# RWKV scan: both products of a block-inversion level over two PSUM banks, and the factor turned by transposes instead of kept twice

## The reference, cut to what matters

```python
def _rwkv7_scan(r, w, k, v, kk, a):
    def step(S, inp):
        r_t, w_t, k_t, v_t, kk_t, a_t = inp
        sa = -jnp.einsum('nhvk,nhk->nhv', S, kk_t)
        S = S * w_t[:, :, None, :] + sa[..., None] * (kk_t * a_t)[:, :, None, :] + v_t[..., None] * k_t[:, :, None, :]
        return S, jnp.einsum('nhvk,nhk->nhv', S, r_t)
    S0 = jnp.zeros((n, h, dk, dk), r.dtype)
    ...
    _, y = lax.scan(step, S0, xs)
```

## Time and profile before

| | us |
|---|---|
| median of 3 runs | 4701.57 |
| lowest and highest | 4696.87, 4706.41 |
| the profiled execution | 4681.85 |
| its span, first to last instruction | 4679.7 |
| granted TensorE clock, mean over the span | 0.946 |

### The profile page before, as it was taken

The page is one execution under the profiler, slowest core; times in us unless marked ns, Lnnn a source line. Parts: engine busy times, 40 slices in busy tenths (PEclk is TensorE's granted clock), DMA queues, the critical chain, the costliest instruction groups (busy, mean ns, idle before and its releaser), DMA issues. The chain is left out here.

```text
span 4679.7 us, 68997 instructions
## 1 busy us (share of the span) xinstructions
PE 4174.6 (89%) x28006; PEld 2421.8 (52%) x28006; DVE 1989.1 (43%) x3941; ACT 1353.8 (29%) x3154; POOL 519.1 (11%) x535
## 2 busy tenths in 40 slices
PE   5999889999998999999997765888798799999994
PEld 2455466644444666445546654777675344433341
DVE  1455256612563565235204665777356222222224
ACT  2125345511144554123113444443141111111110
POOL 0000000000000000000000002322003322222220
PEclk8999999999999999999998886999898899999997
DMA  5122330031222402422011003000304679999995
GB/s 194 46 79 72 105 122 24 31 131 52 91 82 82 132 18 102 158 81 94 26 63 55 2 8 109 3 3 3 117 1 166 241 252 303 309 328 334 333 332 152
DMA packets 199189, 565.69 MB, mean 121 GB/s; under 512 B 24450, under 2 KB 115187, under 8 KB 185427
## 3 DMA queue, kind: packets, MB, share of 16 engines
q1 hardware_dynamic: 162450, 441.90, 26.3%
q0 software_dynamic: 36416, 119.29, 9.3%
HBM read 437.02 MB, written 124.11 MB: 120 GB/s over the span
## 5 line engine op out<-in xcount | busy, mean ns | idle before, releaser
L729 PE MATMUL banks<-arena 128*128 128x512 f32 (+1 forms) x2928 | 1122.3, 540 | 8.1 <-ACT arena L584 5.7
L729 PEld LDWEIGHTS banks<-arena 128*128 128x128 f32 x2928 | 555.3, 191 | 534.1 <-issue 497.8
L3267 PE MATMUL banks<-arena 128*32 128x512 f32 (+2 forms) x2896 | 561.6, 595 | 4.2 <-DMA arena<-in_experts 3.3
L1250 PE MATMUL banks<-arena 128*128 128x256 f32 (+1 forms) x1152 | 375.8, 481 | 18.8 <-DMA arena<-y_d 14.5
L3267 PEld LDWEIGHTS banks<-arena 128*32 128x32 f32 (+2 forms) x2896 | 198.6, 130 | 358.3 <-issue 354.5
L1469 PE MATMUL banks<-arena 96*128 96x512 f32 (+1 forms) x800 | 329.3, 547 | 34.3 <-DMA arena<-k_d 21.1
L1520 DVE TENSOR_REDUCE arena<-banks 128x1 f32<-128x512 f32 (+1 forms) x400 | 226.7, 593 | 294.8 <-PE banks L1469 294.7
L1250 PEld LDWEIGHTS banks<-arena 128*128 128x128 f32 x1152 | 221.4, 193 | 164.5 <-issue 145.2
L3286 PE MATMUL banks<-arena 128*32 128x512 f32 (+2 forms) x1448 | 286.4, 595 | 1.7 <-DVE arena L3316 1.2
L3351 ACT ACTIVATE arena<-banks 128x256 f32<-128x256 f32 x79 | 30.5, 386 | 781.9 <-PE banks L3267 781.9
L3234 POOL DMA_INDIRECT r_d<-arena x125 | 181.5, 1452 | 639.2 <-DVE arena L3316 530.3
(11 more groups left out here) (500 smaller groups left out, 5635.4 us busy)
## 6 DMA issues: line engine op xcount, KB each, us to landing
arena<-in_experts SPq DMA_DIRECT2D x64, 3072.0 KB, 13.2
arena<-in_ada_w SPq DMA_DIRECT2D x12, 2048.0 KB, 7.6
arena<-in_w_in SPq DMA_DIRECT2D x23, 1024.0 KB, 5.6
arena<-in_w_mod SPq DMA_DIRECT2D x8, 2048.0 KB, 17.3
arena<-in_w_out SPq DMA_DIRECT2D x6, 2048.0 KB, 11.4
arena<-in_w_in SPq DMA_DIRECT2D x5, 2048.0 KB, 7.9
arena<-in_tokens SPq DMA_DIRECT2D x4, 2048.0 KB, 17.9
arena<-in_w_mod SPq DMA_DIRECT2D x8, 1024.0 KB, 5.1
```

What stands on the lines that cost most here:

```text
L729: i = e.matmul(self.out_of(n), lhs, rhs, start=k == 0, stop=k == KT - 1)
L1250: i = e.matmul(bank(n % 4)[:, 0:nn], w[:, q, :], H[:, q, t0:t0 + nn], start=q == 0, stop=q == KT - 1)
L3267: op = e.matmul(ABK[(q - q0) % 2][rows, :], xT[(q - q0) % 2][:, P * k:P * k + P][:, rows], weights[:, i % SLOTS, 512 * k:512 * k + 512], s ...
```

## The change

It replaces the pair of factors by one and turns it when needed.

- VectorE keeps only the turned factor `TT_` (256 columns): L2489, L2491 and L2497 work on 256 columns at every level. L2497's result is read from two banks, and its operands are viewed so that the bank index comes first.
- At each level TensorE first transposes `TT_` by two 128x128 transposes, each into columns 128 to 255 of one of the lane's two banks; these wait for the factor, the products behind them also for GpSimd's mask. The eight products with `am` follow, into columns 0 to 127: the chunk (row half) picks the bank, the head's parity the partition half.
- ScalarE's copy takes columns 0 to 255 of both banks at once (128x512 where it was 128x256) into `XN`, which thus holds the product and the plain factor.
- The second product is eight block products for every level (sixteen before, but for the last level), with the row half picking the bank, into columns 256 to 383. The second update is gone.
- X1's product moves from behind the second product of level 2 to behind the first product of level 4, one round later, and writes columns 256 to 511 of both banks, the bank by chunk. Its copy becomes two copies of 64x256, which now stand ahead of the level's copy on ScalarE.
- The uses of the banks are dealt out anew: first and second product each take both banks.

The masks on GpSimd, the Gram products, L2431, L2437 and the chain part are as before, and so is `staged`'s order otherwise.

```diff
--- before.py
+++ after.py
@@ -2321,8 +2321,9 @@
                 self.AB, self.BQ = al(512), al(768)
                 self.AN = self.AB[:, 256:512]
                 self.BT, self.QK_, self.QB = (self.BQ[:, 256 * j:256 * j + 256] for j in range(3))
-                self.TTN, self.XX = al(512), al(256)
-                self.TT_, self.TN = self.TTN[:, 0:256], self.TTN[:, 256:512]
+                self.TT_, self.XN = al(256), al(512)
+                self.banks = [bank(2 * i), bank(2 * i + 1)]
+                self.both = ps[:, 1024 * i:1024 * i + 1024].rearrange("p (two n) -> p two n", two=2)
                 self.am = [al(256), al(256)]
                 self.WT, self.X1, self.UB, self.q1 = (al(256) for _ in range(4))
                 self.WTv = z3(self.WT)
@@ -2335,10 +2336,18 @@
                     for q in range(2):
                         give("gram", n, q, 0), give("gram", n, q, 1)
                     for s_ in LEVELS:
-                        give("x", n, s_), give("tt", n, s_)
-                        if s_ == 2:
-                            give("x1", n)
+                        give("x", n, s_, 0), give("x", n, s_, 1), give("tt", n, s_, 0), give("tt", n, s_, 1)
                     give("wt", n, 0), give("wt", n, 1)
+
+            def product(self, c, h):
+
+                o = 256 * c + 64 * (h // 2)
+                return self.XN[half[h % 2], o:o + 64]
+
+            def factor(self, c, h):
+
+                o = 256 * (h // 2) + 128 + 64 * c
+                return self.XN[half[h % 2], o:o + 64]
 
         lanes = [lane(i) for i in range(3)]
 
@@ -2391,36 +2400,36 @@
                 op.then_inc(Tn.hit("gram", n, gi), 1)
                 yield
             for li, s_ in enumerate(LEVELS):
-                o = sl.of("x", n, s_)
-                sl.free(e, Vn, Sn, "x", n, s_)
                 AM = b.am[li % 2]
+                assert sl.of("x", n, s_, 0) is b.sl.banks[0] and sl.of("tt", n, s_, 0) is b.sl.banks[0]
+                for c in range(2):
+                    sl.free(e, Vn, Sn, "x", n, s_, c)
                 e.wait_ge(*Vn.at("tt", n, li))
+                for g in range(2):
+                    op = e.transpose(b.banks[g][:, P:2 * P], b.TT_[:, P * g:P * g + P], ident)
                 e.wait_ge(*Gn.at("am", n, li))
-                for h in range(4):
-                    hs_ = slice(64 * h, 64 * h + 64)
-                    for tp in half:
-                        op = e.matmul(o[tp, hs_], AM[tp, hs_], b.TT_[tp, hs_], start=True, stop=True)
+                for g in range(2):
+                    for pa in range(2):
+                        hs_ = slice(128 * g + 64 * pa, 128 * g + 64 * pa + 64)
+                        for c, tp in enumerate(half):
+                            op = e.matmul(b.banks[c][half[pa], 64 * g:64 * g + 64], AM[tp, hs_], b.TT_[tp, hs_], start=True, stop=True)
                 op.then_inc(Tn.hit("x", n, li), 1)
-                yield
-                o = sl.of("tt", n, s_)
-                sl.free(e, Vn, Sn, "tt", n, s_)
-                e.wait_ge(*Sn.at("free", "x", n, s_))
-                for lhs, rhs, c0 in ((b.TN, b.XX, 0), (b.XX, b.TN, 256))[0:2 if s_ < 32 else 1]:
-                    for h in range(4):
-                        hs_ = slice(64 * h, 64 * h + 64)
-                        for tp in half:
-                            op = e.matmul(o[tp, c0 + 64 * h:c0 + 64 * h + 64], lhs[tp, hs_], rhs[tp, hs_], start=True, stop=True)
-                op.then_inc(Tn.hit("tt", n, s_), 1)
-                if s_ == 2:
-                    o = sl.of("x1", n)
-                    sl.free(e, Vn, Sn, "x1", n)
+                if s_ == 4:
                     there(e, n)
                     e.wait_ge(*Vn.at("free", "gram", n, 1, 1))
                     for h in range(4):
                         hs_ = slice(64 * h, 64 * h + 64)
-                        for tp in half:
-                            op = e.matmul(o[tp, hs_], b.BT[tp, hs_], v[tp, hs_], start=True, stop=True)
+                        for c, tp in enumerate(half):
+                            op = e.matmul(b.banks[c][tp, 256 + 64 * h:320 + 64 * h], b.BT[tp, hs_], v[tp, hs_], start=True, stop=True)
                     op.then_inc(Tn.hit("x1", n), 1)
+                yield
+                for pa in range(2):
+                    sl.free(e, Vn, Sn, "tt", n, s_, pa)
+                for g in range(2):
+                    for c in range(2):
+                        for pa in range(2):
+                            op = e.matmul(b.banks[pa][half[c], 256 + 64 * g:320 + 64 * g], b.factor(c, 2 * g + pa), b.product(c, 2 * g + pa), start=True, stop=True)
+                op.then_inc(Tn.hit("tt", n, s_), 1)
                 yield
             e.wait_ge(*Vn.at("tt", n, 5))
             for c in range(2):
@@ -2484,17 +2493,18 @@
                     e.tensor_tensor(dst[:, pa], sl.of("gram", n, gi, pa)[:, 0:P * w_].rearrange("p (q g n) -> p q g n", q=w_, g=2), msk, ALU.mult).then_inc(Vn.hit("free", "gram", n, gi, pa), 1)
                 if gi == 0:
                     o_ = CONST + cat["lv1"][0] + (0 if f else 64)
-                    lv = ar[:, o_:o_ + 128].rearrange("p (q n) -> p q n", q=2).unsqueeze(2).broadcast_to([P, 2, 4, 64])
+                    lv = ar[:, o_:o_ + 64].unsqueeze(1).broadcast_to([P, 4, 64])
                     e.wait_ge(*Vn.own())
-                    e.tensor_tensor(b.TTN.rearrange("p (q h n) -> p q h n", q=2, h=4), b.AB.rearrange("p (q h n) -> p q h n", q=2, h=4), lv, ALU.mult).then_inc(Vn.hit(), 1)
+                    e.tensor_tensor(h64(b.TT_), h64(b.AB[:, 0:256]), lv, ALU.mult).then_inc(Vn.hit(), 1)
                     e.wait_ge(*Vn.own())
-                    e.tensor_tensor(h64(b.TTN), cm("id64").unsqueeze(1).broadcast_to([P, 8, 64]), h64(b.TTN), ALU.subtract).then_inc(Vn.hit("tt", n, 0), 1)
+                    e.tensor_tensor(h64(b.TT_), cm("id64").unsqueeze(1).broadcast_to([P, 4, 64]), h64(b.TT_), ALU.subtract).then_inc(Vn.hit("tt", n, 0), 1)
                 yield
             for li, s_ in enumerate(LEVELS):
                 yield
-                w_ = 512 if s_ < 32 else 256
+                tt = b.TT_.rearrange("p (g two n) -> p two g n", g=2, two=2)
                 e.wait_ge(*Tn.at("tt", n, s_))
-                e.tensor_tensor(b.TTN[:, 0:w_], b.TTN[:, 0:w_], sl.of("tt", n, s_)[:, 0:w_], ALU.subtract).then_inc(Vn.hit("free", "tt", n, s_), 1)
+                e.tensor_tensor(tt, tt, b.both[:, :, 256:384].rearrange("p two (g n) -> p two g n", g=2), ALU.subtract).then_inc(Vn.hit("free", "tt", n, s_, 0), 1)
+                Vn.note("free", "tt", n, s_, 1)
                 Vn.note("tt", n, li + 1)
                 yield
             yield
@@ -2529,11 +2539,13 @@
             yield
             for li, s_ in enumerate(LEVELS):
                 e.wait_ge(*Tn.at("x", n, li))
-                e.activation(b.XX, sl.of("x", n, s_)[:, 0:256], ACT.Copy).then_inc(Sn.hit("free", "x", n, s_), 1)
-                yield
-                if s_ == 2:
+                if s_ == 4:
                     e.wait_ge(*Tn.at("x1", n))
-                    e.activation(b.X1, sl.of("x1", n)[:, 0:256], ACT.Copy).then_inc(Sn.hit("free", "x1", n), 1)
+                    for c, tp in enumerate(half):
+                        e.activation(b.X1[tp, :], b.banks[c][tp, 256:512], ACT.Copy).then_inc(Sn.hit("free", "x1", n), 1)
+                e.activation(b.XN.rearrange("p (two n) -> p two n", two=2), b.both[:, :, 0:256], ACT.Copy).then_inc(Sn.hit("free", "x", n, s_, 0), 1)
+                Sn.note("free", "x", n, s_, 1)
+                yield
                 yield
             e.wait_ge(*Tn.at("ub", n))
             for c, tp in enumerate(half):
```

2 lines of the change are left out of this document (1 added, 1 removed).

## The result

The changed kernel is slower: a median of 4724.67 us over 5 runs (4714.95 to 4732.63) against 4701.57 for the kernel before; the ratio is 1.0036, with a 95% interval of 1.0019 to 1.0053. Two later sets of runs beside the kernel before gave 1.0019 (1.0001 to 1.0038) and 1.0039 (1.0024 to 1.0054). I had forecast 36 us less. By the ratios it is some 9 to 18 us more; the three pairs of medians differ by 14 to 23.

The account below looks back on a forecast made before the run. In the scan neither TensorE nor VectorE is full, so a chain of waits between engines bounds it. Six stretches gain 1.9 us of a 21.16 us period, times 19 is 36 us: 4666 us from 4701.6, range 4640 to 4697.

Parts of the forecast that it names:

- The prices: Per-level costs: 0.32 us delay for two transposes, 0.015 us between record starts; VectorE's busy time down 1.6 us an item.
- (d): VectorE through L2468 up to L2378: one more 0.4 us wait beside GpSimd's masks at even odds, minus 0.2 us.
- The sum over a full-clock period: Gains over six stretches of one item's period in the scan: 1.9 us of 21.16.
- (a): VectorE alone from L2654 to the end of L2643: unchanged, 0.
- (b): TensorE from L2606 to L2623: a stall moves to ScalarE's copy behind the sigmoid, leaving a gain of 0.04 us.
- (c): TensorE from L2623 through L2412, then VectorE to L2464: gain of 0.73 us, limited by ScalarE's exponential.
- (e): TensorE from L2378 through L2412 to VectorE's L2497 and L2484: shorter second product, gain of 0.79 us.
- (f): VectorE without a gap to L2654: L2489 and L2491 each 0.27 us shorter, gain of 0.54 us.
- The 19 equal periods: Some 19 periods fit into the scan's 420 us, each gaining 1.9 us: 36 us in all.
- ScalarE's X1 copies ahead of L2514's table load: On ScalarE, about 0.3 us to spare before stalling; part of the stalls-elsewhere rival, chance 0.12.
- The clock: Rival: two falls of TensorE's clock in each scan period, 1.6 us each; 18 us slower, 4720 us; chance 0.10.
- The first rival: ScalarE stalls in more places and GpSimd waits grow: 0.4 us a period left, 8 us, 4694 us; chance 0.12.

Follow-up runs that it names:

- e6: Changed kernel with each level's second product issued twice, plus ScalarE's copy of the second pair of turned keys doubled; one run, scan 443.1 us against 433.8 without the doubled copy.
- e16: Changed kernel with X1's product and its two copies at level 2 in place of level 4; ratio 1.0012 to the kernel before.
- e3: Changed kernel with the second product of each level issued twice, into the same place; ratio 0.9982 to the kernel before.
- e5: Kernel before with the second product updating only the turned factor and VectorE subtracting 256 columns, so the inverse is wrong; ratio 1.0007 to the kernel before.
- e2: Changed kernel, unedited, profiled and timed once more; ratio 1.0019 to the kernel before.
- e11: Kernel before with idle products of 64x64 identities ahead of each group of key transposes; ratio 0.9995 to the kernel before.
- e7: Changed kernel with each level's second product issued twice, and the second group of Gram products twice as well; ratio 1.0037 to the kernel before.
- e8: Kernel before with the second group of Gram products issued twice, into the same places; ratio 1.0013 to the unedited kernel before.
- e9: Changed kernel with idle products of 64x64 identities ahead of each group of key transposes; ratio 1.0024 to the kernel before.
- e13: Changed kernel with idle 128x128 transposes ahead of the key transposes and spare identity products in the first two items; ratio 1.0025 to the kernel before.
- e14: Second run of the changed kernel with idle 128x128 transposes ahead of the key transposes; ratio 1.0008 to the kernel before.
- e10: Changed kernel with idle 128x128 transposes ahead of each group of key transposes; ratio 1.0018 to the kernel before.

## Why the prediction was wrong, by its steps

**The prices were right.** L2409 at 3084.10 to L2415 at 3084.47 is 0.37 for two transposes (I had 0.32), L2415's 16 records take 0.46, which is 0.016 between starts (0.015), L2546 is 0.58 to 0.60, L2506 and L2498 are 0.42. VectorE's busy time in the scan fell by 24.6 us, 1.2 an item, where I had 1.6; most of the rest is in (d). The four-corner pattern with a bank for each row half does what I took it to do.

**The sum over a full-clock period** came out at 0.8 us (21.1 to 20.3), not 1.9. By stretches, from the rows above against the earlier trace rows:

- (a) L2666 to L2618: 2.88 against 3.01, a gain of 0.13 for my 0.
- (b) L2618 to L2635: 5.32 against 5.32; I had 0.04. The stall did move to ScalarE: L2431 at 3086.19 waits 0.57 for L2546, which stands behind the sigmoid.
- (c) L2635 to L2473: 4.77 against 5.44, 0.67 for my 0.73.
- (d) L2473 to the second L2387: 2.96 against 2.50, a loss of 0.46 for my 0.2. L2474, which took its plain 0.41 in the kernel before, now takes 0.94, as L2475 does. It is just past the end of my range. In the kernel before GpSimd's two masks stood apart, and this instruction (3056.52) began between them; now they run from 3093.01 to 3094.78 without a break, beside L2474 and the start of L2475. That they cause it fits these times but wasn't tried. The Trainium skill (SBUF — State Buffer, Who interferes with whom) says that a VectorE instruction with two SBUF inputs contends with a GpSimd instruction that reads SBUF; the doubled length agrees.
- (e) the second L2387 to L2493: 2.16 against 2.36, a gain of 0.20 for my 0.79. **This step failed.** I let the first Gram products start as soon as the shortened second product was over. They write the two banks that the key transposes wrote, so they wait for ScalarE's copies of both; L2399 at 3096.95 waits 0.39 us for L2536. Before, the 0.9 us of L2412 covered that copy, so shortening it could give no more than 0.2. I had asked what hides each edit's cost but not what the removed work had hidden. e6 shows the copy on the path.
- (f) L2493 to L2666: 2.01 against 2.53, 0.52 for my 0.54.

The six give 0.13 + 0 + 0.67 - 0.46 + 0.20 + 0.52 = 1.06 us for this pair of periods; the mean over full periods is 0.8.

**The 19 equal periods were the second failed step.** Six of the 19 are start, in which items have no chain end. There the change loses 8.0 us on the mean (118.8, 118.3, 116.2 against 111.1, 108.4). I had a rival for that mechanism, ScalarE's X1 copies ahead of L2514's table load with 0.3 us to spare, and gave it a chance only in the steady part, where it hardly counts. e16 shows it: 4 to 7 us of the 8 go when X1's product and copies come a level earlier.

**The clock was the third.** I gave the rival that ends slower 0.10, at 1.6 us a fall. In the traces of the changed kernel the clock is low in 9 to 13 of the 13 steady periods instead of 4. That the fewer records do it is shown by e3, which gives them back and has 2, and with less force by e5 (33 us of low clock for 14, in 5 periods). Two periods of the changed kernel, one full and one with a clock of 0.81; as the low level is half of the full one, that is (1 - 0.81) x 2 x 22.24 = 8.5 us of low clock:

```profile
2995.71:3016.16 20.45, 15.75 (x412) 12.26 (x407) 14.67 (x34) 10.13 (x20) 6.02 (x8) 1.00 0.01 3
3140.67:3162.91 22.24, 18.80 (x398) 14.80 (x396) 14.51 (x33) 10.13 (x20) 5.97 (x8) 0.81 0.01 2
```

The second has the same work and is 1.8 us longer (columns as in the earlier trace rows). So of the 0.8 x 13 = 10 us that the steady part should have gained, 6 were left in two traces (280.0 to 274.4), and e2 lost 4 (283.7). I had the place of the falls wrong: I put them behind the wait for L2654. They begin in the stretch of the key transposes; even the one that I named, at 3101, lies 18 us behind the L2491 at 3083.17. Filling that stretch took them away (e11), and filling another one (e7, e8) didn't help. I also counted four where the trace of the kernel before has three more, near 2950, 3165 and 3230. I also argued against it that the period shrinks with the work. It didn't shrink enough: the waits stayed and the work went.

Together, the scan: start +8.0, steady part -2.5 on the mean of three traces, head and tail of the scan +2.1, in all +7.6 us, where I forecast -36. The first rival, ScalarE's stall in more places, and the clock both came about; I had priced them as alternatives, and they add up.

What stays open: how much more than 7.6 us the change costs in timed runs, since the routing stage spreads by 35 us from trace to trace, by the clock of the router's products and by one long wait, and the change may or may not bear on either; why the spells of e9, e13 and e14 come in some traces and hardly in e10's; and whether GpSimd is what VectorE waits for in (d).

## What to carry to other kernels

When an edit takes work off an engine that is woven with others, list what that work was covering (a copy, a drain, another engine's queue), since each of these becomes the new end; a gain is the smallest of the margins. Price the fill and the steady part of a software pipeline apart, because work that is covered in one stands bare in the other. And where TensorE runs with gaps, look at the granted clock by stretch before and after: here an empty stretch, not the mean load, decided, and 0.24 us of repeated products a level at the right place were worth some 13 us of the scan.

## What the runs showed of the hardware

Idle work held TensorE's clock up when it stood in the stretch where the clock fell. Identity products in waits of 0.44 and 0.57 us took the steady part of the kernel before from four low periods to none (280 to 273.6 us, e11); the second Gram group computed twice, in another stretch, left five and made it 291 (e8). 128x128 transposes did there what products of 64x64 blocks did: with either no fall begins at the key transposes in the steady part. The Trainium skill (TensorE: Matmul & The Clock Gate, Part 4) says that transposes don't count as busy for the clock as products do; here, in fp32, no such difference shows: 12 and 7 of 13 steady periods are full with transposes (e10, e14) and 9 with products (e9), where the changed kernel has 4 or none. The routing stage, the same code in all kernels, took 161 to 199 us: the same 128 router products 15 us or, at a low clock, 27, and in 11 of 20 traces one wait of 15 to 26 us that by the code is for the landing of a store.
